# Attention stage: each head's two prompt tiles taken between its two groups of sample tiles

## The reference, cut to what matters

```python
q = _apply_rope(_rmsnorm(q.reshape(B, T, 8, 128), q_norm), cos, sin)
k = _apply_rope(_rmsnorm(k.reshape(B, T, 2, 128), k_norm), cos, sin)
...
def block(qi):                      # 128 queries of every head
    s = jnp.einsum('bqhgd,bkhd->bhgqk', qi, k).astype(jnp.float32) * scale
    p = jax.nn.softmax(s, axis=-1).astype(v.dtype)
    return jnp.einsum('bhgqk,bkhd->bqhgd', p, v)
...
y_prompt = _trunk(x_prompt, params)   # 256 tokens
y_sample = _trunk(x_sample, params)   # 1024 tokens
```

## Time and profile before

| | |
|---|---|
| median of three runs | 3561.52 us |
| the profiled execution | 3566.13 us, its span 3564.3 us |
| granted TensorE clock, mean over the span | 0.975 |
| TensorE matmul busy | 3347.8 us, 94% of the span |
| VectorE busy | 1833.8 us, 51% |
| ScalarE busy | 990.2 us, 28% |
| attention loop | from 242.3 us to 552.1 us of the span |

### The profile page before, as it was taken

How to read it: one execution, slowest core, us unless ns; L and a number is a source line. 1 busy time by engine, 2 the same in 40 slices (tenths; PEclk the granted TensorE clock), 3 DMA queues, 4 the chain that set the end, 5 groups by cost and what they waited for, 6 DMA issues and landing times. The chain is left out here.

```text
span 3564.3 us, 57177 instructions
## 1 busy us (share of the span) xinstructions
PE 3347.8 (94%) x24648; PEld 2149.8 (60%) x24648; DVE 1833.8 (51%) x3086; ACT 990.2 (28%) x1570; POOL 2.5 (0%) x13
## 2 busy tenths in 40 slices
PE   9999997999999599889999899999899999999997
PEld 4565554454555355568888745556666666666665
DVE  2347762476776478035555423126564454654546
ACT  2334431333433223223333345000321111122121
POOL 0000000000000000000000000000000000000000
PEclk9999999999999799999999999999999999999999
DMA  3210000253453422253443232111112121122211
GB/s 130 67 28 16 15 20 32 72 175 114 136 183 101 164 82 98 106 182 119 131 141 120 99 132 83 67 62 71 47 60 77 60 83 53 60 77 89 83 59 60
DMA packets 199146, 316.53 MB, mean 89 GB/s; under 512 B 50672, under 2 KB 156144, under 8 KB 193776
## 3 DMA queue, kind: packets, MB, share of 16 engines
q1 hardware_dynamic: 198896, 312.87, 25.5%
HBM read 211.26 MB, written 95.03 MB: 86 GB/s over the span
## 5 line engine op out<-in xcount | busy, mean ns | idle before, releaser
L629 PE MATMUL ra_ps<-xT,ra_w 128*128 128x512 f32 (+1 forms) x1152 | 432.0, 528 | 18.8 <-DMA ra_w<-in_w_in 18.0
L629 PEld LDWEIGHTS ra_ps<-xT,ra_w 128*128 128x128 f32 x1152 | 215.1, 191 | 219.4 <-issue 191.4
L1656 PE MATMUL tl_ps<-merged,tl_sums 128*128 128x320 f32 x1088 | 322.3, 436 | 15.3 <-DVE oR L1849 7.8
L997 PE MATMUL rg_ps<-xT,rg_w 128*128 128x512 f32 (+1 forms) x768 | 287.3, 530 | 17.2 <-DMA rg_w<-in_w_gate 17.2
L1849 DVE TENSOR_TENSOR oR<-tl_ps,oR 128x320 f32<-128x320 f32 x416 | 201.9, 489 | 151.6 <-PE tl_ps L1656 149.4
L1656 PE MATMUL tl_ps<-merged,tl_wt 128*128 128x320 f32 x896 | 270.5, 437 | 8.9 <-DMA tl_wt<-in_w_out 8.9
L1656 PEld LDWEIGHTS tl_ps<-merged,tl_sums 128*128 128x128 f32 x1088 | 206.3, 191 | 109.5 <-issue 28.1
L1656 PE MATMUL tl_ps<-tl_Th,tl_sums 128*128 128x320 f32 x864 | 241.2, 436 | 8.4 <-issue 6.1
L997 PEld LDWEIGHTS rg_ps<-xT,rg_w 128*128 128x128 f32 x768 | 145.6, 193 | 138.5 <-issue 115.2
L1656 PEld LDWEIGHTS tl_ps<-merged,tl_wt 128*128 128x128 f32 x896 | 171.9, 192 | 81.4 <-DMA tl_wt<-in_w_out 9.3
L1656 PEld LDWEIGHTS tl_ps<-tl_Th,tl_sums 128*128 128x128 f32 x864 | 165.5, 192 | 78.5 <-issue 11.1
(11 more groups left out here) (236 smaller groups left out, 4710.1 us busy)
## 6 DMA issues: line engine op xcount, KB each, us to landing
rc_ub<-ub SPq DMA_DIRECT2D x80, 640.0 KB, 5.2
ub<-ra_ub SPq DMA_DIRECT2D x32, 1280.0 KB, 5.3
tl_wt<-in_w_ff SPq DMA_DIRECT2D x32, 1024.0 KB, 4.7
tl_wt<-in_w_ff SPq DMA_DIRECT2D x64, 512.0 KB, 3.2
ra_w<-in_w_in SPq DMA_DIRECT2D x24, 512.0 KB, 3.3
ub<-ra_v SPq DMA_DIRECT2D x16, 640.0 KB, 6.1
gates<-rg_gate SPq DMA_DIRECT2D x16, 640.0 KB, 3.7
mg_gate<-gates SPq DMA_DIRECT2D x16, 640.0 KB, 3.9
```

Of the source, the lines that this page charges most:

```text
L629: last = pe.matmul(ps[:, bank + j, 0:n], w[c][:, 128 * i:128 * i + 128], xT[:, i, t0:t0 + n], start=(i == 0), stop=(i == KT - 1))
L997: last = pe.matmul(ps[:, 3 * (b % 2) + j, 0:n], w[b % 3][:, 128 * i:128 * i + 128], xT[:, i, t0:t0 + n], start=(i == 0), stop=(i == KT - 1))
L1656: last = pe.matmul(bank(n, b), lhs(k), rhs(k), start=(fresh and k == 0), stop=(k == d - 1), skip_group_check=True)
```

## The change

The list of groups is put in another order. Before, it holds all 16 sample groups, head by head, and then the 8 prompt groups. Now each head has its first sample group, its prompt group and its second sample group in a row. Nothing else differs: the same tiles, the same instructions for each tile, the same buffers and rules.

```diff
-        GROUPS = [(h, 512 * i, 0, SEQ_S, 4) for h in range(QH) for i in range(2)] + [(h, SEQ_S, SEQ_S, SEQ_P, 2) for h in range(QH)]
+        GROUPS = [group for h in range(QH) for group in
+                  ((h, 0, 0, SEQ_S, 4), (h, SEQ_S, SEQ_S, SEQ_P, 2), (h, 512, 0, SEQ_S, 4))]
```

## The result

The changed kernel takes 3582.01 us (median of 6 runs, 3578.74 to 3587.54), beside 3559.73 us for the kernel before (6 runs, 3557.0 to 3565.84): +22.3 us, a ratio of 1.0062 with a 95% interval of 1.0049 to 1.0075. It is slower, inside the range of 3565 to 3585 and 4.6 us above the time that was forecast. The profiled execution took 3578.74 us, its span 3576.9, against 3566.13 and 3564.3 before: +12.6.

A forecast was written before the change was run, and what follows sets the result against it. TensorE, busy 94% of the span, was taken as the bound, with only the attention loop able to change. 13.65 + 0.6 + 1.7 = +15.9 us took the median from 3561.52 to 3577.4 us, range 3565 to 3585.

The forecast's parts named there:

- The ring: Attention loop, VectorE and ScalarE: a sample tile without enough values work beside it takes 3.55 us.
- One head: Attention loop, from one head's second prompt tile to the next's: 39.06 us for 36.65 of TensorE work, 2.41 lost.
- First and last head: Ends of the attention loop: 1.3 us lost in the first head, about 4.1 in the last, with a 2.6 us wait.
- The prompt waits of before: Prompt tiles of the kernel before: 13 TensorE waits, some 8.5 us, which the change can win.
- The clock: Last head: TensorE's clock falls behind the 2.6 us wait, costing +1.7 us, with 0 to 3.4 possible.
- rival 4: TensorE's clock falls in every head's second sample group: +10.5 to +12 us more, some 3588; chance 0.08.
- Rival 1: Last head: same as the forecast, but the clock doesn't fall: +14.2 us, 3575.7; chance 0.27.
- The tail: End of the attention stage: last output 512 columns wide, not 256, so copy and DMA take +0.6 us.
- The sum: Whole kernel: 13.65 to the last output copy, 0.6 for the wider output, 1.7 for the clock: +15.9 us.
- Rival 2: Second sample group: VectorE and ScalarE's lead from the prompt tiles carries over four tiles: -6.6 us, 3554.9; chance 0.05.
- Rival 3: Second sample group: only VectorE's own work, 2.9 us a sample tile, bounds it: about +1 us, 3562.5; chance 0.11.

The follow-up runs named there:

- e7: Changed kernel with the scaling covering only the first 256 of a sample tile's 1024 columns; median +2.6 us against before, ratio interval 0.9997 to 1.0020.
- e4: Changed kernel with a third buffer for transposed probabilities and a list spreading values matmuls over tiles; median 3558.89 us, 7.0 us below before.
- e5: Changed kernel with the last head's two last groups swapped (sample, sample, prompt); median +10.3 us against before.
- e2: Changed kernel with group order altered: each head takes both sample groups, then its prompt group; median +6.7 us against before.
- e6: Changed kernel with prompt groups taken after every second head (four sample groups, then two prompt groups); median +5.4 us against before.
- e1: The changed kernel measured again, unaltered; median +17.3 us against before, recorded ratio 1.0056.
- e3: Kernel before with 21 useless matmuls added at the end of the attention stage, shifting later stages; median +18.2 us against before.
- e8: Kernel before with 42 useless matmuls added at the end of the attention stage, shifting later stages; median +31.3 us against before.

## Why the prediction was right

**The ring.** Said: a sample tile without enough values work takes 3.55 us. Measured: 3.54, and 3.15 when 0.40 was taken out (e7).

**One head.** Said, from the start of the second prompt tile: 5.38, 8.07, 11.87, 15.42, 18.96, and 39.06 to the next. Measured: 272.74, 275.42, 279.23, 282.77 and 286.31 less 267.37 are 5.37, 8.05, 11.86, 15.40 and 18.94, and the head is 39.04.

**First and last head.** Said: last prompt tile of the first head at 267.63, that of the last at 541.05, the last sample tile 15.42 later and 2.6 us late. Measured: 267.37 (the loop had begun 0.3 earlier), 540.64, 556.04 and 2.45 by the view.

**The prompt waits of before.** Said: 8.5 us. e4, which removes them and pays only the first head's 1.3, is 7.0 shorter, so 8.3.

**The clock.** Said: a fall in the last head, 1.7 us. It fell, in both traces of the changed kernel. The copy stands 566.24 - 556.04 = 10.20 behind the last tile's transposes, where 24.3 - 15.42 = 8.9 were worked out at full clock and e7 has 9.05 at full clock: the fall cost 1.2. The size was 0.5 too high, and that the clock fell at all was in part luck (see the last section). In the middle heads the clock did not fall, so rival 4 is out. Rival 1 is out for the traces seen. In e5, which lacks the one long wait and keeps the short ones of seven heads, the clock doesn't fall.

**The tail.** Said: 0.6. From the last output copy to the next stage's first matmul it is 7.52 before (551.70 to 559.22) and 7.99 after: 0.5. That alone shows little, since this time lies between 7.38 and 8.63 over the eight kernels without a shift. The part up to the first load of `lr_w` is steady: 3.24 to 3.30 us where the last output is 256 columns wide (before, e2, e5, e6), 3.80 to 3.82 where it is 512 wide (both of the changed kernel, e4, e7). So 0.55 is the wider output, and the rest of the scatter is that of the load.

**The sum.** Said 13.65 + 0.6 + 1.7 = 15.9. Measured to the handover 15.0: 14.8 in the loop and 0.5 behind it, less 0.3 by which this loop began earlier. Of the 0.9 that lack, 0.5 is the price of the clock and 0.3 the earlier start. Rival 2 (the lead carries over four tiles) fell at the point that was named: the maximum of the third sample tile waits for scores that stand behind the first tile's transposes (275.54 above). The lead lasts for one tile, and the second comes 2.68 us after it, 0.08 late. That rival read rows 1 as two regimes in which the busiest engine changes; they don't show that, for TensorE is the busiest in both (31.79 us against VectorE's 25.97 in the second), and there it waits on VectorE. Interleaving the two did pay in e4, once the values work was moved too. Rival 3 fell as rows 6 had said: VectorE's own work doesn't set the pace, since it stands idle 0.67 us in each turn for the exponential (281.76 above).

**The size.** By the medians of the first runs the total is 6 us more than forecast, by those of e1 1.4 us more (4 by its recorded ratio). The forecast lies just below the interval of the first set (17.4 to 26.7 us) and inside that of the second (14 to 25). The kernel before itself has medians of 3559.7 and 3565.9 on the two occasions. That, with the rest column, makes the scatter of executions the likely reason; it is not shown to be the only one.

## What to carry to other kernels

When TensorE is always busy, ask of every tile what it would cost without the filler work beside it: here a sample tile needs 3.55 us around the ring and is free only as long as its matmuls take longer, as the 4.31 us of the old order did. Mixing short and long tiles moves the filler (the values product of the group before) away from the tiles that need it, because each group's filler is spread over the next group whatever that group's size. With the filler spread by need, and one more buffer to let it wait, the mixed order here was 7.0 us faster than the old order as it stood.

## What the runs showed of the hardware

TensorE's clock after one and the same wait fell in some executions and not in others. All kernels but e7 run the same instructions up to the first scaling at some 248 us, for which TensorE waits 2.36 us. In before, after, e1, e3 and e5 the scores behind it ran at half clock, and in e2, e4, e6 and e8 they did not. Rows 9 show the kernel before, where the scores took 3.38; this is e6, where they took 1.88:

```profile
249.82 1.09 PE L290 MATMUL at_ps<-cst,at_p 128*128 128x128 f32 x8 [2.37 <-DVE at_p L428]
250.75 1.88 PE L280 MATMUL at_ps<-at_qk 128*128 128x512 f32 x4
```

The wait of 2.47 us at 215 us had the same two outcomes: a clock of 0.79 over 214 to 222 us in seven of the ten traces, 1.00 in e2, e4 and e8. From the first scores to the transposes of 259.91 it is 17.65 us in before and 16.15 in e8, so this fall costs 1.5; in the changed kernel it is 17.85, so 1.7. From the end of the wait at 215 us to the first scores it is 25.3 us in the three traces without a fall there and 26.8 to 27.0 in the seven with one: again 1.5 to 1.7. With up to 2.0 us that come from before this wait (it ends at 214.71 to 216.72), the two falls move this place of the same program from 256.2 to 260.3 us.

In the attention loop, shorter waits did not bring a fall in any of these traces. The nearest ones are 2.05 and 1.97 us in e7, and 2.02 us at the fourth tile of the first group wherever a prompt group follows it (changed kernel, e1, e4, e5), as in this row of the changed kernel; the clock is 1.00 from 259 us on:

```profile
259.61 1.09 PE L289 MATMUL at_ps<-cst,at_p 128*128 128x128 f32 x8 [2.02 <-DVE at_p L427]
```

The fall in the last head (wait of 2.45 us) was put down as likely because both waits of that size in one trace had it. Over all traces such waits have it in five of nine cases at 248 us, in seven of ten at 215 us and in two of two in the last head. So a second outcome of the same kernel, without the 1.2 us, would have been no surprise.
